# Prompt attention scores from float32r products of stacked high and low parts, in a hybrid decode-step layer

## The chip, the core and the metric

The kernel runs on one core of a Trainium2 chip. The metric is the device time of one execution in microseconds; the median of three runs is given. Engines are named as the profile names them: PE is TensorE, DVE is VectorE, ACT is ScalarE, POOL is GpSimd, SP is SyncE.

## What is computed

One transformer layer, for a prompt of 1024 tokens and for 8 sequences that each add one token to a past of 2048. The width is 1024, the feed-forward width 2816. Half of the mixer is attention with 8 query heads of 64 in 2 key groups, the other half a retention. Attention has three branches per query: compressed blocks, selected blocks, and a window of 512. For the prompt the reference does this, a block of queries at a time:

```python
qg = q.reshape(Sq, KV_GROUPS, HPG, HEAD_DIM)
s_c = jnp.einsum('sghd,ngd->sghn', qg, kcb).astype(jnp.float32) * scale
p_c = masked_softmax(s_c, (blk_end[None, :] <= q_pos[:, None])[:, None, None, :])
o_c = jnp.einsum('sghn,ngd->sghd', p_c.astype(vcb.dtype), vcb)
...
s_s = jnp.einsum('sghd,sgkd->sghk', qg, k_g).astype(jnp.float32) * scale
...
s_w = jnp.einsum('sghd,wgd->sghw', qg, kw).astype(jnp.float32) * scale
...
o = g[..., 0:1] * o_c + g[..., 1:2] * o_s + g[..., 2:3] * o_w
```

At 1024 tokens the prompt has no more selected blocks than the branch may take, so the selected branch sees every key up to the query's own. Everything is float32.

## The kernel before

Six blocks run one after another; at the end of each all engines meet at a barrier. Within a block every engine has its own instruction list, written out by hand, with semaphore counts between them.

1. `stage_project` (twice: retention columns, then keys, values and queries) multiplies the normalised rows by the input weights. Products there are "split": each float32 operand is kept as a float32r high part and a float32r rest, and `split_products` (line 374) issues three products per piece. The turned queries `qT` (4 pairs of heads x 128 rows x 1024 tokens) and keys `kselT`, `kwinT` stay in SBUF. The queries' group 0 lies in rows 0 to 63, group 1 in rows 64 to 127.
2. `stage_sequences` does the 8 single tokens. It first compresses the prompt's rows to 63 blocks (`kcbP`, `vcbP`), with weights `w1`, `w2`.
3. `stage_attention` does the prompt. Its work is 192 units in the order (tile of 128 queries, head pair, group, branch). PE's list is `EVENTS_C`: S is a unit's scores, three units ahead; T turns its exponents; V multiplies them by values; E and F close a tile. Per unit DVE takes the row maximum from PSUM, ACT writes the exponents, DVE and ACT in turn copy the turned blocks. A branch has one score area in PSUM.
4. `stage_mix_out` and `stage_feed_forward` follow, with split products throughout.

For the scores of one head, `pad_queries` copies the group's 64 rows into `qz`, whose other 64 rows are zero, so that one fp32 product over 128 rows with the keys of both groups gives the group's scores (line 1471). The masks are added by a bf16 product (line 1474). Scores are cut into pieces at PSUM banks and at the 128 columns that have a mask: for a tile t the selected branch has 128 x (t + 1) columns, the window at most 640, the compressed one 63.

```python
for lo, hi, mask in pieces(i):
    last = pe.matmul(out[:, lo:hi], m.qz[t % 2][:, hh, g, :], keys[:, lo:hi], start=True, stop=not mask)
    if mask:
        add = {"cmp": m.cmpb16[:, t, :], "causal": m.causalb, "edge": m.edgeb}[mask]
        last = pe.matmul(out[:, lo:hi], m.identb, add, start=False, stop=True)
```

`prepare_attention` runs on POOL at the end of block 2: masks to bf16, zeros, and the queries of tiles 0 and 1. Later tiles' queries are padded by POOL during block 3. In block 3 SP only loads `w_out` and the row `ln2`, for block 4. `rest_to_lo` (line 383) subtracts the high part from a float32 source; `round_to_hi` (line 379) writes the high part.

Of the kernel before, what the change touches and what calls it, by code (L numbers as in the profile page):

```python
# [16 lines left out]
F32 = mybir.dt.float32  # L17
# [44 lines left out]
KEPT = 8 * SEQ + 64 + NT * GW + 8 + 24 + 192  # L62
# [6 lines left out]
def constants():  # L69
# [23 lines left out]
    n = np.arange(63)  # L93
    put("cmp", np.stack([np.where(n[None, :] * CH + 31 <= t * P + p[:, None], 0, NEG) for t in range(TP)], 1))
# [16 lines left out]
class Semaphores:  # L111
# [5 lines left out]
    def __getitem__(self, name):  # L117
        if name not in self.by_name:
            self.by_name[name] = self.ctx.enter_context(self.nc.semaphore(name))
# [97 lines left out]
def place_kept(nc, ctx, m):  # L217
# [3 lines left out]
    m.qT = room(4 * SEQ).rearrange("p (h t) -> p h t", h=4)  # L221
    m.qbd = room(64).rearrange("p (b r) -> p b r", b=8)
    m.kselT, m.kwinT = room(SEQ), room(SEQ)
# [5 lines left out]
    m.kcbP, m.vcbP = room(64), room(128)  # L229


def place_keys(nc, ctx, m):
# [5 lines left out]
    m.qp = [m.lnb[:, 512 * i:512 * i + 512] for i in range(2)]  # L238


def place_mixer(nc, ctx, m):

    arena = ctx.enter_context(nc.sbuf_tensor("arena", [P, WORDS - CORE - KEPT], F32))
    room = Room(arena, 0)
    place_constants(m, room(NCONST - N_LATE), N_LATE)
    m.identb, m.causalb, m.edgeb = (room(P // 2).bitcast(BF16) for _ in range(3))
    m.cmpb16 = room(TP * 32).bitcast(BF16).rearrange("p (t n) -> p t n", t=TP)[:, :, 0:63]
# [13 lines left out]
    m.w2 = [b(128).rearrange("p (m n) -> p m n", m=2) for _ in range(2)]  # L261
    m.posT = [b(16) for _ in range(2)]
# [16 lines left out]
    m.rst = x(72)  # L279

# [5 lines left out]
    c = Room(arena, after_const)  # L286
    m.prob = [c(1024) for _ in range(4)]
    m.qz = [c(8 * P).rearrange("p (h g t) -> p h g t", h=4, g=2) for _ in range(2)]
# [3 lines left out]
    m.sums, m.rsc, m.nmax = [c(24), c(24)], c(24), c(8)  # L292

# [92 lines left out]
TURN_STEPS = (3, 6)  # L386


def stage_project(nc, s, m, io, first, end):
# [19 lines left out]
    with nc.Block() as block:  # L409

        @block.sync
        def _(sp):
# [13 lines left out]

            def load_x(i):
# [3 lines left out]
            if first == 0:  # L431
                load_x(0)
                sp.dma_start(m.ident, io.const[:, 0:P]).then_inc(s["ident_in"], 16)
                sp.dma_start(m.lnb, io.ln1[0:1, :].to_broadcast((P, DM))).then_inc(s["ln1_in"], 16)
# [10 lines left out]
            for n in range(n0, n1):  # L445
# [130 lines left out]
        def _(dve):  # L576
# [20 lines left out]
            if first == 0:  # L597
                dve.memset(m.small[:, 64:65], EPS).then_inc(s["a_dve_const"], 1)
                dve.wait_ge(s["ln1_in"], 16)
# [205 lines left out]
def pad_queries(pool, s, m, t):  # L805

    if t >= 2:
# [1233 lines left out]
```

## Time and profile before

| what | value |
|---|---|
| median of three runs | 2213.86 us (2211.0 to 2223.89) |
| the profiled execution | 2213.31 us, its span 2211.6 us |
| PE, PEld (weight loads) busy | 95%, 82% of the span |
| DVE, ACT, POOL busy | 35%, 27%, 21% |
| mean granted PE clock | 0.974 of full |
| line 1471 (scores), PE busy | 161.2 us, 720 records |
| line 1500 (values), line 1488 (turns) | 172.9 us, 109.7 us |
| line 374 (split products) | 855.8 and 349.7 us, 6696 records |

Busy time of PE adds up durations that overlap at their ends, so a record's duration is longer than its turn on the engine. The attention block runs from about 940 to 1316 us of the span. Its eight tiles begin their first exponent at 941.4, 957.8, 986.0, 1019.8, 1062.2, 1116.7, 1175.9 and 1238.4 us.

### The profile page before, as it was taken

To read this page: it belongs to the slowest core of one execution; us is meant where nothing else is said; L and a number is where in the kernel's file an instruction comes from. 1 tells how busy PE (TensorE), PEld (TensorE's weight loads), DVE (VectorE), ACT (ScalarE), POOL (GpSimd) and SP (SyncE) were. 2 spreads that over 40 slices of the span, in tenths; PEclk is the share of its full clock that TensorE was granted. 3 is DMA by queue.
4 is the path that set the end of the run, shared out by engine and by line. 5 is a ranking of instruction groups with operands and counts; after the bars stand their busy time and mean duration, and the time that the engine had idled before them with its cause. 6 is when DMAs were issued, how large, how long until landed. Compare 5 with 4: busy or idle time off the path is not lost. (4 is left out here: it accounts for less than half of the span.)

```text
span 2211.6 us, 34591 instructions
## 1 busy us (share of the span) xinstructions
PE 2095.4 (95%) x12669; PEld 1812.5 (82%) x12669; DVE 772.1 (35%) x1454; ACT 599.4 (27%) x1269; POOL 459.7 (21%) x433
## 2 busy tenths in 40 slices
PE   6999989978999999699999989899999999999998
PEld 5777768856776777488888868699999999999987
DVE  5544433554344444455444453301111011111015
ACT  4310112112333333265444442222110111111112
POOL 0111112212223321210000002133321333223330
PEclk9999989988999999699999989999999999999999
DMA  5211102047886773020000002121111111111123
GB/s 176 68 58 39 39 26 84 30 103 123 112 108 103 100 100 52 24 68 1 1 1 1 1 29 106 66 75 43 45 48 47 48 47 43 43 51 44 45 69 116
DMA packets 159455, 131.89 MB, mean 60 GB/s; under 512 B 15257, under 2 KB 147050, under 8 KB 159010
## 3 DMA queue, kind: packets, MB, share of 16 engines
q1 hardware_dynamic: 155234, 121.85, 23.7%
q0 software_dynamic: 4096, 8.40, 2.2%
q8 instruction: 76, 1.25, 0.2%
q14 instruction: 49, 0.40, 0.1%
HBM read 117.85 MB, written 16.55 MB: 61 GB/s over the span
## 5 line engine op out<-in xcount | busy, mean ns | idle before, releaser
L374 PE MATMUL banks<-halves 128*128 128x344 f32 (+4 forms) x5184 | 855.8, 327 | 12.6 <-POOL halves L383 12.6
L374 PEld LDWEIGHTS banks<-halves 128*128 128x128 f32 (+1 forms) x5184 | 821.2, 188 | 43.1 <-issue 7.5
L383 POOL TENSOR_TENSOR halves<-core,halves 128x1024 fp32r<-128x1024 f32 (+1 forms) x143 | 243.8, 1712 | 641.4 <-ACT halves L379 491.4
L374 PE MATMUL banks<-hidden 128*128 128x512 f32 (+3 forms) x1512 | 349.7, 387 | 9.1 <-DVE hidden L383 9.1
L374 PEld LDWEIGHTS banks<-hidden 128*128 128x128 f32 (+1 forms) x1512 | 254.7, 179 | 77.6 <-issue 9.7
L1017 PE MATMUL banks<-arena 128*128 128x254 f32 (+1 forms) x1152 | 248.4, 372 | 11.2 <-ACT arena L1148 7.1
L1017 PEld LDWEIGHTS banks<-arena 128*128 128x128 f32 x1152 | 208.8, 194 | 37.4 <-issue 6.2
L379 ACT ACTIVATE halves<-core 128x1024 fp32r<-128x1024 f32 (+1 forms) x85 | 88.1, 1047 | 388.4 <-PE banks L374 369.6
L1929 DVE TENSOR_TENSOR core<-banks,core 128x344 f32<-128x344 f32 x66 | 34.0, 516 | 440.6 <-PE banks L374 440.6
L1500 PE MATMUL banks<-kept,arena 128*128 128x64 f32 (+1 forms) x1184 | 172.9, 277 | 6.4 <-ACT arena L1532 4.2
L1500 PEld LDWEIGHTS banks<-kept,arena 128*128 128x128 f32 (+1 forms) x1184 | 151.1, 191 | 20.6 <-issue 16.9
L1471 PE MATMUL banks<-kept,arena 128*128 128x128 f32 (+4 forms) x720 | 161.2, 342 | 0.9 <-PEq L849 0.9
L1517 ACT ACTIVATE arena<-banks,arena 128x63 f32<-128x63 f32 (+8 forms) x192 | 109.5, 571 | 166.9 <-DVE arena L1570 149.7
L1570 DVE TENSOR_REDUCE arena<-banks 128x1 f32<-128x640 f32 (+4 forms) x184 | 102.4, 558 | 128.1 <-PE banks L1474 126.4
L1471 PEld LDWEIGHTS banks<-kept,arena 128*128 128x128 f32 x720 | 116.6, 192 | 32.6 <-issue 16.2
L930 POOL DMA_DIRECT2D arena<-in_cache_kv x128 | 67.8, 530 | 235.4 <-PE banks L1058 209.7
L1488 PE MATMUL banks<-core,arena 128*128 128x128 f32 (+1 forms) x592 | 109.7, 280 | 0.2 <-ACT arena L1517 0.2
L561 POOL TENSOR_TENSOR retention<-core,retention 128x256 f32<-128x256 f32 (+1 forms) x36 | 30.3, 841 | 261.4 <-ACT core L544 261.4
L1576 DVE COPY arena<-banks 63x128 f32<-63x128 f32 (+4 forms) x129 | 59.5, 461 | 62.3 <-PE banks L1488 61.2
L1148 ACT ACTIVATE arena<-banks 128x512 f32<-128x512 f32 (+1 forms) x72 | 39.7, 577 | 147.5 <-PE banks L998 147.0
L629 DVE TENSOR_TENSOR retention<-core,retention 128x128 f32<-128x128 f32 (+1 forms) x72 | 37.6, 564 | 119.9 <-ACT core L544 119.9
L1880 ACT ACTIVATE core<-banks 128x344 f32<-128x344 f32 x66 | 30.2, 458 | 175.1 <-PE banks L374 175.0
(203 smaller groups left out, 1791.2 us busy)
## 6 DMA issues: line engine op xcount, KB each, us to landing
core<-in_cache_kv SPq DMA_DIRECT2D x128, 128.0 KB, 5.5
core<-in_w_gate SPq DMA_DIRECT2D x22, 512.0 KB, 3.8
core<-in_w_up SPq DMA_DIRECT2D x22, 512.0 KB, 3.7
core<-in_x_prompt SPq DMA_DIRECT2D x16, 512.0 KB, 3.4
arena<-in_cache_kv SPq DMA_DIRECT2D x128, 64.0 KB, 5.1
arena<-in_cache_kv POOLq DMA_DIRECT2D x128, 64.0 KB, 3.9
retention<-in_w_in SPq DMA_DIRECT2D x16, 448.0 KB, 6.2
core<-in_w_down SPq DMA_DIRECT2D x16, 448.0 KB, 3.6
```

Source lines behind the costliest of these rows:

```text
L374: done = pe.matmul(out, left[a], right[b], start=(first and i == 0), stop=(last and i == 2))
L379: return act.activation(hi, x, ACT.Copy)
L383: return engine.tensor_tensor(lo, x, hi.bitcast(F32), ALU.subtract)
L930: pool.dma_start(m.selv[16 * at:16 * at + 16, half, :, :], io.pool[bass.ds(page[pg], 1), :, :, 384:512].rearrange("a c t n -> (a c) t n")) ...
L1017: last = pe.matmul(m.banks[:, 2 + mt, 0:2 * nb], m.w1[kv][:, k, P * mt:P * mt + P], m.XT[:, k % 8, :, k // 8:k // 8 + nb], start=(k == 0), ...
L1148: act.activation(m.XT.rearrange("p (h j) g c -> p j h g c", h=2)[:, i, :, :, 0:nch], m.banks[:, u % 2, :].rearrange("p (g c h) -> p h g c" ...
L1471: last = pe.matmul(out[:, lo:hi], m.qz[t % 2][:, hh, g, :], keys[:, lo:hi], start=True, stop=not mask)
L1488: last = pe.transpose(m.banks[0:w, 5 + i % 2, P * x:P * x + P], m.prob[u % 4][:, P * (first + x):P * (first + x) + w], m.ident)
L1500: last = pe.matmul(m.banks[:, 7, HD * (u % 8):HD * (u % 8) + HD], m.pts[i % 3][0:w, P * x:P * x + P], v[0:w, 64 * g:64 * g + 64], start=(f ...
L1517: act.activation(m.prob[i % 4][:, 0:width(i)], scores_of(i, width(i)), ACT.Exp, bias=m.nmax[:, i % 8:i % 8 + 1], accum_out=m.sums[UNITS[i] ...
L1570: dve.tensor_reduce(peak, out, AX.X, ALU.max, negate=True).then_inc(s["c_max"], 1)
L1576: dve.tensor_copy(m.pts[i % 3][0:w, 0:P * n], m.banks[0:w, 5 + i % 2, 0:P * n]).then_inc(s["c_kept_dve"], 1)
```

## The change

The score product of a piece becomes two float32r products. The stationary operand `qs` holds, for one head, the query's high part in rows 0 to 63 and its rest in rows 64 to 127. The moving operand is once the group's keys' high part, in both halves of the rows, and once their rest, in both halves. The two add up in PSUM to (high + rest) x (high + rest). The zero rows and `qz` go.

To lay queries and keys out in both halves, the projection block stores `qT`, `kselT` and `kwinT` to DRAM (`turned_queries`, `turned_keys`), and later blocks read them back, each group's 64 rows into both halves. Keys come in at the end of block 2 (`kstage`), queries per tile in block 3 (`qstage`). ACT writes the high parts, DVE the keys' rests, POOL the queries' rests (64 rows). The compressed keys are made in both halves by `w2twice`, which holds `w2` two times side by side. Because more semaphores are needed, 35 names that only the projection uses are cleared and freed after it, followed by a barrier of all engines. The compressed branch is 64 columns wide instead of 63. The mask casts stay on POOL; the padding there goes.

```diff
+    def retire(self, names):
+        self.nc.clear_and_free_semaphores([self.by_name.pop(name) for name in names])
+        self.nc.all_engine_barrier()
...
@@ stage_project, SP
+            def store_queries(t):
+                sp.dma_start(io.turned_queries[:, :, t * P:(t + 1) * P].rearrange("h p t -> p h t"),
+                             m.qT[:, :, t * P:(t + 1) * P]).then_inc(s["turned_out"], 16)
...
+                if ch in (5, 6) and t == 2:
+                    sp.wait_ge(s["tkept"], turns_before(n))
+                    sp.dma_start(io.turned_keys[ch - 5], (m.kselT, m.kwinT)[ch - 5]).then_inc(s["turned_out"], 16)
+                if kind == "q" and t >= 2:
+                    sp.wait_ge(s["tkept"], turns_before(n - 1))
+                    store_queries(t - 2)
...
+                sp.wait_ge(s["tkept"], turns_before(NI - 1))
+                store_queries(TP - 1)
                 sp.wait_ge(s["gate_done"], NT)
                 sp.dma_start(io.gate_rows, m.gates[0:NB_SEQ, TP, :]).then_inc(s["rows_out"], 16)
                 sp.wait_ge(s["rows_out"], 32)
+                sp.wait_ge(s["turned_out"], 16 * (2 + TP))
...
@@ stage_sequences, SP
                 sp.dma_start(m.w2[kv], io.w2[kv]).then_inc(s[f"b_w_in{kv}"], 16)
+                if kv == 0:
+                    for half in range(2):
+                        sp.dma_start(m.w2twice[:, :, HD * half:HD * half + HD], io.w2[0]).then_inc(s["b_w_in0"], 16)
...
+            sp.wait_ge(s["b_grouped"], 2 * (NB_SEQ + 1))
+            for what in range(2):
+                for g in range(2):
+                    for half in range(2):
+                        sp.dma_start(m.kstage[what][g][HD * half:HD * half + HD, :],
+                                     io.turned_keys[what, HD * g:HD * g + HD, :]).then_inc(s["c_keys_in"], 16)
...
@@ stage_sequences, POOL
-            prepare_attention(pool, s, m)
+            pool.wait_ge(s["const_in"], 48)
+            for b16, f32 in stored_masks(m):
+                pool.tensor_copy(b16, f32).then_inc(s["c_masks"], 1)
+            pool.wait_ge(s["c_masks"], 4)
...
@@ stage_attention, SP
+            def load_queries(t):
+
+                for g in range(2):
+                    src = io.turned_queries[:, HD * g:HD * g + HD, P * t:P * t + P].rearrange("h d t -> d h t")
+                    for half in range(2):
+                        sp.dma_start(m.qstage[t % 2][HD * half:HD * half + HD, g, :, :], src
+                                     ).then_inc(s[f"c_q_in{t % 2}"], 16)
+
+            for t in range(2):
+                load_queries(t)
+            sp.wait_ge(s["c_keys_lo"], 4)
             for k in range(NSLOT):
                 load_w_out(sp, s, m, io, k)
+            for t in range(2, TP):
+                sp.wait_ge(s["c_queries"], t - 1)
+                load_queries(t)
...
@@ stage_attention, PE
-                    pe.wait_ge(s["c_queries"], 2 * t + 2)
+                    pe.wait_ge(s["c_queries"], t + 1)
+                    if t == 0 and hh == 0 and br:
+                        pe.wait_ge(s["c_keys_lo"], 2 * g + br)
...
                     for lo, hi, mask in pieces(i):
-                        last = pe.matmul(out[:, lo:hi], m.qz[t % 2][:, hh, g, :], keys[:, lo:hi], start=True, stop=not mask)
+                        for v in range(2):
+                            last = pe.matmul(out[:, lo:hi], m.qs[t % 2][:, g, hh, :], pair[v][:, first + lo:first + hi],
+                                             start=(v == 0), stop=(v == 1 and not mask))
...
@@ stage_attention, ACT
+            def queries_hi(t):
+
+                act.wait_ge(s[f"c_q_in{t % 2}"], 64 * (t // 2 + 1))
+                wait(act, "c_scores", PER_TILE * (t - 1))
+                round_to_hi(act, m.qs[t % 2], m.qstage[t % 2]).then_inc(s["c_q_hi"], 1)
+
+            queries_hi(0)
+            act.wait_ge(s["c_keys_in"], 128)
+            for g in range(2):
+                for what in range(2):
+                    round_to_hi(act, m.keys[what][g][0], m.kstage[what][g]).then_inc(s["c_keys_hi"], 1)
+            queries_hi(1)
...
+                    t = i // PER_TILE + 1
+                    if i % PER_TILE == 4 and 2 <= t < TP:
+                        queries_hi(t)
                     act.wait_ge(s["c_max"], i + 1)
...
@@ stage_attention, POOL
+            def queries_lo(t):
+
+                pool.wait_ge(s["c_q_hi"], t + 1)
+                low = slice(HD, P)
+                rest_to_lo(pool, m.qs[t % 2][low], m.qstage[t % 2][low], m.qs[t % 2][low]).then_inc(s["c_queries"], 1)
+
+            queries_lo(0)
+            pool.wait_ge(s["c_queries"], 1)
+            queries_lo(1)
+            for t in range(TP - 1):
+                if t:
+                    pool.wait_ge(s["c_weighted"], t)
+                    queries_lo(t + 1)
...
@@ stage_attention, DVE
+            for g in range(2):
+                for what in range(2):
+                    dve.wait_ge(s["c_keys_hi"], 2 * g + what + 1)
+                    rest_to_lo(dve, m.keys[what][g][1], m.kstage[what][g], m.keys[what][g][0]).then_inc(s["c_keys_lo"], 1)
             for what, i in EVENTS_C:
...
@@ build, after stage_project
+            s.retire(PROJECT_ONLY)
```

## Rows read from the trace of the kernel before

**Rows 1.** Stretches of the span by engine; us, busy us (records), granted clock, DMA.
```profile
918.00:928.00 10.00, 0.91 (x8) 0.58 (x7) 8.61 (x12) 3.38 (x5) 6.83 (x9) 0.61 0.01 5
...
936.00:940.00 4.00, 3.23 (x23) 2.11 (x21) 0.60 (x3) 0.00 (x0) 0.00 (x0) 0.85 0.00 0
941.00:957.80 16.80, 16.23 (x139) 14.09 (x138) 10.18 (x44) 12.61 (x62) 0.77 (x2) 1.00 0.81 220
1238.40:1303.50 65.10, 64.52 (x469) 53.84 (x467) 30.56 (x47) 28.12 (x69) 2.76 (x1) 1.00 0.00 1
```

**Rows 2.** Groups by shape, TensorE, attention stage: records, busy us, mean ns.
```profile
L1471 PE MATMUL banks<-kept,arena 128*128 128x128 f32 x368 | 67.5, 276 | 0.0
...
L1471 PE MATMUL banks<-kept,arena 128*128 128x384 f32 x112 | 47.1, 502 | 0.0
...
L1471 PE MATMUL banks<-kept,arena 128*128 128x512 f32 x64 | 32.8, 594 | 0.0
...
L1471 PE MATMUL banks<-kept,arena 128*128 128x63 f32 x128 | 21.4, 249 | 0.9 <-PEq L849 0.9
...
L1471 PE MATMUL banks<-kept,arena 128*128 128x256 f32 x48 | 14.3, 380 | 0.0
```

**Rows 3.** Timeline, three stretches of TensorE: start, us, operation, records merged.
```profile
1273.08 0.19 PEld L1471 LDWEIGHTS banks<-kept,arena 128*128 128x128 f32 x1 [0.24 <-issue]
1273.51 0.51 PEld L1471 LDWEIGHTS banks<-kept,arena 128*128 128x128 f32 x2 [0.24 <-issue]
...
1107.37 1.28 PE L1500 MATMUL banks<-kept,arena 128*128 128x64 f32 x10
1108.49 0.28 PE L1488 MATMUL banks<-core,arena 128*128 128x128 f32 x1
...
336.93 5.80 PE L374 MATMUL banks<-hidden 128*128 128x512 f32 x24
342.56 0.27 PE L738 MATMUL banks<-core 128*128 128x128 f32 x1
```

**Rows 4.** Stretches, line 374 alone: 344 columns, then 256; busy us (records).
```profile
1500.00:1550.00 50.00, 50.00 (x320) 50.00 (x319) 1.00 0.18 52
...
2158.00:2161.00 3.00, 3.00 (x26) 3.00 (x27) 1.00 0.00 0
```

**Rows 5.** Line 374's weight loads: records, ns min/median/max, shapes.
```profile
L374 PEld LDWEIGHTS banks<-halves x5184: 87/188/338, 1321.1 to 2197.2; 128*128 128x128 f32 x198, 128*8 128x8 f32 x2
```

**Rows 6.** Timeline, first maximum and SyncE's first issues of the attention stage.
```profile
940.93 0.22 DVE L1567 TENSOR_REDUCE arena<-banks 128x1 f32<-128x63 f32 x1 [0.95 <-PE banks L1474]
...
940.26 4.98 SPq L1420 DMA_DIRECT2D core<-in_w_out  x8
```

**Rows 7.** Issues by line: count, KB each, median us from issue to landing.
```profile
arena<-in_cmp_w_k SPq DMA_DIRECT2D x8, 256.0 KB, 3.9
```

**Rows 8.** Timeline, the same splitting operations on three engines, next stage's start.
```profile
1316.52 7.68 ACT L379 ACTIVATE halves<-core 128x1024 fp32r<-128x1024 f32 x8 [0.29 <-PEq L1451]
...
1317.61 1.22 DVE L383 TENSOR_TENSOR halves<-core,halves 128x1024 fp32r<-128x1024 f32 x1 [3.25 <-ACT halves L379]
1319.50 4.89 DVE L383 TENSOR_TENSOR halves<-core,halves 128x1024 fp32r<-128x1024 f32 x3 [0.67 <-ACT halves L379]
...
1318.60 2.44 POOL L383 TENSOR_TENSOR halves<-core,halves 128x1024 fp32r<-128x1024 f32 x1 [68.56 <-ACT halves L379]
```

**Rows 9.** Timeline, end of the projection stage and the next stage's first issue.
```profile
450.64 0.68 DVE L652 TENSOR_SCALAR kept<-banks 128x512 f32<-128x512 f32 x1
...
457.98 0.39 DVE L656 TENSOR_SCALAR kept<-banks 64x32 f32<-64x32 f32 x2 [0.75 <-PE banks L738]
458.66 0.24 SPq L853 DMA_DIRECT2D arena<-in_page_table  x1
```

**Rows 10.** Groups by line: one operation in 905 to 940, and the whole span.
```profile
L1332 DVE TENSOR_SCALAR core<-core 8x30 f32<-8x30 f32 x1 | 1.7, 1691 | 0.0
...
L1332 DVE TENSOR_SCALAR core<-core 8x30 f32<-8x30 f32 x8 | 6.9, 858 | 0.3
```

More of the change, by code:

```diff
@@ L92, in constants @@
     put("edge", np.where(i[None, :] > p[:, None], 0, NEG))
-    n = np.arange(63)
-    put("cmp", np.stack([np.where(n[None, :] * CH + 31 <= t * P + p[:, None], 0, NEG) for t in range(TP)], 1))
+    n = np.arange(64)
+    put("cmp", np.stack([np.where((n[None, :] < 63) & (n[None, :] * CH + 31 <= t * P + p[:, None]), 0, NEG)
+                         for t in range(TP)], 1))
     r = np.arange(NRANK)
@@ L228, in place_kept @@
     m.gs = room(24).rearrange("p (b n) -> p b n", b=8)
-    m.kcbP, m.vcbP = room(64), room(128)
+    m.vcbP = room(128)
+    m.identb, m.causalb, m.edgeb = (room(P // 2).bitcast(BF16) for _ in range(3))
+    m.cmpb16 = room(TP * 32).bitcast(BF16).rearrange("p (t n) -> p t n", t=TP)
+    m.kcbP = ctx.enter_context(nc.sbuf_tensor("kept_pairs", [P, CMPK], F32R, side="right"))[:, :].rearrange(
+        "p (g v n) -> p g v n", g=2, v=2)
 def place_keys(nc, ctx, m):
@@ L279, in place_mixer @@
     m.rst = x(72)
+    m.kstage = [[m.pool[:, 2048 * a + 1024 * g:2048 * a + 1024 * g + 1024] for g in range(2)] for a in range(2)]
     m.S0, m.S2, m.rsq = scores[:, 0:4096], sel, sel[:, 0:1024]
@@ L283, in place_mixer, with place_attention @@
     m.R4 = m.kwb[:, 0:256].rearrange("p (j e) -> p j e", j=4)
-    c = Room(arena, after_const)
+def place_attention(nc, ctx, m):
+    room = Room(ctx.enter_context(nc.sbuf_tensor("pairs", [P, PAIRS_C], F32R)), 0)
+    m.keys = [[[room(SEQ) for _ in range(2)] for _ in range(2)] for _ in range(2)]
+    m.qs = [room(SEQ).rearrange("p (g h t) -> p g h t", g=2, h=4) for _ in range(2)]
+    c = Room(ctx.enter_context(nc.sbuf_tensor("softmax", [P, WORDS - CORE - KEPT - CMPK - PAIRS_C], F32)), 0)
     m.prob = [c(1024) for _ in range(4)]
-    m.qz = [c(8 * P).rearrange("p (h g t) -> p h g t", h=4, g=2) for _ in range(2)]
+    m.qstage = [c(SEQ).rearrange("p (g h t) -> p g h t", g=2, h=4) for _ in range(2)]
     m.pts = [c(512) for _ in range(3)]
@@ L292, in place_mixer @@
     m.sums, m.rsc, m.nmax = [c(24), c(24)], c(24), c(8)
+    m.kstage = [[m.pool[:, 2048 * a + 1024 * g:2048 * a + 1024 * g + 1024] for g in range(2)] for a in range(2)]
 def place_feed_forward(nc, ctx, m):
@@ L386 @@
 TURN_STEPS = (3, 6)
+PROJECT_ONLY = ("x_in0", "x_in1", "ident_in", "aw_in", "aw_hi", "aw_lo", "turned", "hT_hi", "hT_lo", "h_done", "rms_done",
+                "raw_done", "roped", "tkept", "tturned", "cos_done", "proj_done", "vkept", "w_used", "att_done",
+                "att_masked", "kd_done", "o_done", "state_done", "state_out", "gates_kept", "gates_late", "gate_done",
+                "turned_out", "rows_out") + tuple(f"slot_out{k}" for k in range(5))
 def stage_project(nc, s, m, io, first, end):
@@ L1433, in width @@
     def width(u):
-        return 63 if UNITS[u][3] == 0 else P * key_tiles(u)
+        return 64 if UNITS[u][3] == 0 else P * key_tiles(u)
     def pieces(u):
@@ L1543, in _ @@
         def _(pool):
[L1544 to L1549 removed]
+            def queries_lo(t):
[9 more added lines that the diff above has]
+                    queries_lo(t + 1)
+                pool.wait_ge(s["c_queries"], t + 2)
                 pool.wait_ge(s["c_inverted"], t + 1)
@@ L2014, in build @@
                     stage_project(nc, s, m, io, 4, NCH)
-            place_mixer(nc, kept, m)
-            stage_sequences(nc, s, m, io)
-            stage_attention(nc, s, m, io)
+            s.retire(PROJECT_ONLY)
+            with ExitStack() as part:
+                place_mixer(nc, part, m)
+                stage_sequences(nc, s, m, io)
+            with ExitStack() as part:
+                place_attention(nc, part, m)
+                stage_attention(nc, s, m, io)
         place_feed_forward(nc, ctx, m)
```

96 lines of the change are left out of this document (49 added, 47 removed).

## The prediction

> **What bounds the kernel now.** I read first the stretches of the span by engine, because the change touches four stages and a price holds only in its own stage. The last tile of the prompt's attention, 1238.4 to 1303.5, is the picture to keep [rows 1]: TensorE is busy 64.52 of 65.10 us at the full clock, VectorE 30.56 and ScalarE 28.12. So in this stage a shorter TensorE instruction shortens the stage, and ScalarE and VectorE have about half their time free. At the stage's head and tail another thing decides: the chain from the first scores to the first maximum, and what must be ready before them.
>
> **The score products.** By shape, the stage has 720 records of line 1471 [rows 2]. There are 360 products in the code, so an fp32 product runs as two records, each with its own weight load. After the change each piece is two float32r products, which run as one record each (line 374 has 5184 records for the 5184 float32r products that its loops issue). The count of records and loads stays 720; only the length of a record changes.
>
> The length is the distance between starts, not the duration, because records overlap. Two neighbouring loads of 512-column fp32 records start at 1273.08 and 1273.51: 0.43 us apart [rows 3]. By columns that is 0.323 for 384, 0.216 for 256, and 0.108 for 128. For float32r, 24 records of 512 columns fill the 5.63 us from 336.93 to the next group at 342.56, 0.235 each [rows 3]; 320 records in 50 us, of 344 columns, are 0.156, and 26 in 3 us, of 256, are 0.115 [rows 4]. Between 344 and 512, 384 columns come to 0.175.
>
> - 512 columns: 64 x (0.43 - 0.235) = 12.5 us
> - 384 columns: 112 x (0.323 - 0.175) = 16.6 us
> - 256 columns: 48 x (0.216 - 0.115) = 4.8 us
>
> The 128-column records, 368 of them, are the unknown: float32r at 128 columns does not occur before. By stream alone it would take 0.235/4 = 0.059 instead of 0.11. But an fp32 record of 64 columns streams as long as a float32r record of 128, and ten of those fill the 1.12 us from 1107.37 to 1108.49: 0.112 [rows 3]. Something other than the stream sets that floor; the load is the candidate, since a float32r load lasts 188 ns with 128 columns and 87 with 8 [rows 5], about 0.10 us for the columns. I take 0.11, no gain, by that nearest row; the ends are 0.059 (368 x 0.052 = 19 us more gained) and, if load and stream followed one another, 0.10 + 0.059 = 0.16 (18 us lost). The 63-column records (now 64 columns) go with them.
>
> The Trainium skill has a rule that speaks against the change: TensorE: Matmul & The Clock Gate, in its part on packing small matmuls ("The mechanism"), says that a weight load overlaps matmuls in flight only when it targets another row group, and these all use the whole array. By it no load here would be hidden, and the change would lose time. The 0.156 us of 344 columns contradicts it: load 0.10 and stream 0.235 x 344/512 = 0.158 would add up to 0.26. I go by the row, and keep the rule as a rival.
>
> Sum of the wide records: 33.9 us. Not all will show: where scores come back sooner, some steps will end on an exponent or a copy. With two engines at half load I take 31; the ends are 33.9 and half.
>
> **The start of the attention stage.** Before, the first maximum runs at 940.93, 0.67 us after SyncE's first issue of the stage at 940.26 [rows 6]; queries were padded by GpSimd under the sequences' tail. Now the chain starts inside the stage. Four query loads of 128 KB go first on SyncE. Eight issues took 4.98 us there, 0.62 apart [rows 6], so the fourth goes out at 942.1; 256 KB landed 3.9 us after issue [rows 7]: 946.0. ScalarE rounds eight 1024-column slices in 7.68 us in the stage after [rows 8], 0.95 apart: queries until 947.1, four key parts until 950.9, the second tile's queries until 951.9. GpSimd's rest of 1024 columns takes 2.44 [rows 8], so 949.5 and 954.3. VectorE has four key rests to do before its first maximum, in program order: 1.22 each, but the one that met GpSimd's ended 1.1 after GpSimd did, and three took 4.89 instead of 3.7 [rows 8]. The first rest meets the first queries' (ends 950.6), the second and third end at 953.0, the fourth meets the second tile's queries or not: 954.2 to 956.4. Against 940.93 that is 13.3 to 15.5 us late; I take 14. The first scores are earlier than that (951); maxima, exponents and turns are what is late.
>
> Meanwhile TensorE is idle. Before, it had nearly no work from 918 to 928 (0.91 us busy); the granted clock was 0.61 on average there and still 0.85 in 936 to 940 [rows 1]. So once it had fallen from 2.4 to 1.2 GHz, it came back only some 8 us after the work did. Tile 0 keeps TensorE occupied: 139 records x 0.11 = 15 of its 16.8 us [rows 1], so 8 us at half clock cost at most 4, some of it in its gaps: 3 us. Nothing excludes 0 or 5.
>
> **The rest.**
> - ScalarE rounds the queries of six more tiles, 0.95 each, one place before an exponent; ScalarE is free for half the tile [rows 1], so most is hidden; uncovered, it is 6 x 0.95 = 5.7. I take 1. GpSimd's part runs a tile ahead; SyncE's query loads wait for GpSimd two tiles earlier and hold up only w_out and the ln2 row, which nothing needs until the next stage.
> - Project stage: SyncE stores turned keys and queries in its queue. Behind its waits stand the prompt rows (needed only in the next stage) and the gate rows. The last query tile is copied at 451.3 (450.64 + 0.68), the stage's last copy ends at 458.4 (457.98 + 0.39) [rows 9]; a 256 KB store, issue and the 3.9 us of [rows 7], lands by 456. Hidden, by 2 us; without that cover, 2 to 4 us.
> - Clearing 35 semaphores, and one more barrier: the trace shows none; the next row is a stage change, 458.37 to the next issue at 458.66 [rows 9], 0.3 us. I take five of that, 1.5, with ends at one and ten, 0.3 and 3.
> - Sequences: two more w2 loads ahead of the position rows and of w1 of the values: 2 x 0.5 us of issue, partly hidden: 0.5. The 2 MB of keys are read once GpSimd has grouped the last rows and SyncE has sent the last window values, under the last sequence's softmax; without that cover they would be late by up to their own landing time. GpSimd's padding leaves VectorE's last chain, in which one 8x30 operation took 1691 ns [rows 10], against 858 on average over eight with that one in it: -0.9 us.
>
> Sum: -31 + 14 + 3 + 1 + 0 + 1.5 + 0.5 - 0.9 = -11.9 us. The profiled execution took 2213.31 (its span 2211.6 and 1.7 around it), against a median of 2213.86: 2201.4 us, and I say 2201. Half a per cent, 11 us, is about what a measurement of this kernel can tell from no change.
>
> **Rivals.**
> A. The sum, with a start between 11 and 20 us in all and the gain between 28 and 34: 2192 to 2209. Chance 0.58.
> B. The narrow records quicken too, because the float32r load is shorter than its duration says: 19 us more, 2182. Against it stands the 64-column row. 0.10.
> C. TensorE stops being the bound: score, maximum, exponent in turn set the pace, and only half of the 33.9 comes: 2201 + 14 = 2215. For it: at 1024 columns maximum and exponent follow one another, and one bank group serves each branch. Against it: half-idle engines, and three units' work between a score and its turn. 0.12.
> D. The clock stays at half through tile 0 and into tile 1: some 12 us more, 2213. For it: the start is thinner than the tail in which the clock fell before. 0.11.
> E. The other side: weight loads are not hidden under float32r records here. Each record then costs 0.10 plus its stream: 64 x 0.095 + 112 x 0.048 + 48 x 0.001 - 368 x 0.05 = -7 us, and the 128 of 64 columns lose 0.02 each against 0.11, 3: the products lose 10 instead of gaining 31, 2242. It decides for slower from about 0.03 us of load showing per record (23 us over 720). Spacing at 344 columns speaks against it. 0.09.
>
> **How the numbers follow.** A lies below 2203 in about two thirds: 0.38, with B 0.48 faster; the rest of A with C and D, 0.43, is within 0.5%; E, 0.09, slower. The range takes in A, C, D and part of B: 2186 to 2217.
>
> **What would show it.** Two float32r records per piece, 720, with 512 columns 0.23 apart and 128 columns 0.11; the first maximum 14 to 16 us after the stage's first issue; half clock in the first tile; tiles 4 to 7 each 5 to 8 us shorter, tiles 0 and 1 no shorter but for their start. The prediction is wrong if narrow records stand at 0.06 or 0.16, if late tiles shrink by less than 3 us, or if the first maximum comes after 20 us.

## The result, and the profile after

The changed kernel takes 2225.55 us (median of 20 runs, 2222.85 to 2233.49) against 2213.72 for the kernel before (20 runs): a ratio of 1.006, 95% interval 1.005 to 1.0071, so 12 us slower, where 2201 had been forecast. The profiled execution took 2224.61 us, its span 2222.9, its mean granted clock 0.954 (0.974 before).

The first thing to read is where in the span the two kernels part. Each tile runs here from its first exponent to the next tile's (the last tile to its last exponent), in us:

| stretch | before | after | difference |
|---|---|---|---|
| end of projection to first issue of the sequences | 0.28 | 3.24 | +3.0 |
| end of the sequences' last group of eight products to the first exponent | 2.36 | 16.82 | +14.5 |
| tile 0 | 16.4 | 26.4 | +10.0 |
| tile 1 | 28.2 | 45.1 | +16.8 |
| tile 2 | 33.8 | 34.3 | +0.5 |
| tiles 3 to 7 together | 283.7 | 252.8 | -30.9 |

The rest is projection (+1.2), sequences (-3.2) and what follows the last exponent (-0.6). The first two move as much from one execution to the next: in the profiled executions below, of either kernel's code, projection ends between 457.3 and 459.6 and the sequences last 474.5 to 481.6 us.

So the late tiles gained what had been said, the start lost what had been said, and two tiles in which nothing was to be won or lost but the 3 us of the clock lost 27. Stretches of the changed kernel, to be read against [rows 1] (span of the stretch, busy us and records of PE, PEld, DVE, ACT and POOL, granted clock, DMA):

```profile
940.00:945.00 5.00, 0.22 (x1) 0.13 (x1) 0.59 (x3) 0.00 (x0) 0.00 (x0) 1.00 0.30 88
945.00:950.00 5.00, 0.19 (x1) 0.22 (x2) 1.78 (x1) 3.82 (x5) 2.34 (x1) 0.50 0.41 122
...
956.80:983.20 26.40, 25.97 (x131) 24.33 (x132) 10.31 (x42) 13.37 (x62) 0.00 (x0) 0.50 0.66 160
983.20:1028.30 45.10, 45.10 (x222) 43.01 (x221) 15.48 (x41) 18.32 (x65) 5.11 (x2) 0.50 0.04 12
1028.30:1035.00 6.70, 6.70 (x35) 6.47 (x34) 2.33 (x7) 2.60 (x9) 0.00 (x0) 0.50 0.01 4
1035.00:1062.60 27.60, 27.60 (x240) 26.56 (x239) 14.90 (x32) 18.18 (x59) 5.12 (x2) 0.96 0.07 20
1256.20:1315.40 59.20, 57.80 (x466) 54.86 (x465) 30.53 (x47) 28.12 (x69) 2.76 (x1) 0.97 0.00 1
```

The clock falls to half (0.50, 1.2 GHz) at 945, while TensorE waits, and is still there at 1035. Through tile 1 and the head of tile 2 TensorE is busy without a gap (45.10 of 45.10, 6.70 of 6.70), and VectorE and ScalarE are less busy per microsecond than before. In tile 1 nothing is waited for: the same 222 records take 45.1 us in place of the 28.2 of the kernel before:

```profile
957.80:986.00 28.20, 26.95 (x222) 24.51 (x221) 14.74 (x41) 16.16 (x64) 4.13 (x4) 0.94 0.00 1
```

By the 0.96 from 1035 on the clock is back at about 1037, 92 us after it fell. Tile 7 at 59.2 against 65.1 is the change as it was meant.

The start, by the timeline of the same kernel, answers to [rows 6, 8]:

```profile
941.19 5.22 SPq L1507 DMA_DIRECT2D softmax<-turned_queries  x8
946.18 1.06 ACT L398 ACTIVATE pairs<-softmax 128x1024 fp32r<-128x1024 f32 x1 [18.51 <-DMA softmax<-turned_queries]
947.14 3.88 ACT L398 ACTIVATE pairs<-core 128x1024 fp32r<-128x1024 f32 x4
947.32 2.34 POOL L402 TENSOR_TENSOR pairs<-softmax,pairs 64x1024 fp32r<-64x1024 f32 x1 [23.70 <-ACT pairs L398]
948.22 8.08 DVE L402 TENSOR_TENSOR pairs<-core,pairs 128x1024 fp32r<-128x1024 f32 x4 [7.29 <-ACT pairs L398]
949.81 0.61 PE L1535 MATMUL banks<-kept_pairs,pairs 128*128 128x64 f32 x2 [9.27 <-POOL pairs L402]
...
956.33 0.23 DVE L1659 TENSOR_REDUCE softmax<-banks 128x1 f32<-128x64 f32 x1
```

The first maximum stands 15.1 us after SyncE's first issue, behind the four rests that VectorE takes in program order; TensorE waits 9.27 us for the queries and, behind the first scores, another 4.4 for the first exponent.

The score records of the whole stage by shape (records, busy us, mean ns) answer to [rows 2]:

```profile
L1535 PE MATMUL banks<-pairs 128*128 128x128 f32 x368 | 76.0, 306 | 0.7 <-DVE pairs L402 0.7
...
L1535 PE MATMUL banks<-pairs 128*128 128x384 f32 x112 | 33.0, 376 | 0.0
...
L1535 PE MATMUL banks<-kept_pairs,pairs 128*128 128x64 f32 x128 | 28.9, 312 | 9.3 <-POOL pairs L402 9.3
...
L1535 PE MATMUL banks<-pairs 128*128 128x512 f32 x64 | 23.0, 440 | 0.0
```

With the 48 of 256 columns the counts are the 720 that were expected, shape by shape. 512 columns went from 594 to 440 ns and 384 from 502 to 376; 128 columns went from 276 to 306, a mean that holds the half-clock tiles too.

At the stage change behind the projection, timeline again, against [rows 9]:

```profile
457.98 0.67 DVE L688 TENSOR_SCALAR turned_rows<-banks 128x512 f32<-128x512 f32 x1
458.68 0.36 SPq L451 DMA_DIRECT2D turned_queries<-turned_rows  x1
...
459.08 0.40 SPq L513 DMA_DIRECT2D gate_rows<-kept  x1
459.21 0.39 DVE L692 TENSOR_SCALAR kept<-banks 64x32 f32<-64x32 f32 x2 [0.56 <-PE banks L774]
462.84 0.25 SPq L870 DMA_DIRECT2D arena<-in_page_table  x1
```

The last query tile leaves VectorE at 458.65, not at 451.3, and its store is issued 4.2 us before the next stage can begin.

### The profile page after: what moved, and what is told of

Read it like the earlier page. It is cut to its first block and busy times, and to the rows that moved or that the text cites. A ratio compares the mean times of both kernels' runs of the same rounds, so it can differ in the third digit from the quotient of the medians.

```text
span 2222.9 us, 34694 instructions
## 1 busy us (share of the span) xinstructions
PE 2093.9 (94%) x12669; PEld 1844.6 (83%) x12669; DVE 779.3 (35%) x1460; ACT 613.2 (28%) x1282; POOL 469.1 (21%) x424
## 5 line engine op out<-in xcount | busy, mean ns | idle before, releaser
L1565 PE MATMUL banks<-kept,softmax 128*128 128x64 f32 (+1 forms) x1184 | 188.2, 293 | 6.1 <-ACT softmax L1612 4.3
L1565 PEld LDWEIGHTS banks<-kept,softmax 128*128 128x128 f32 (+1 forms) x1184 | 166.7, 208 | 15.6 <-issue 8.2
L1597 ACT ACTIVATE softmax<-banks,softmax 128x64 f32<-128x64 f32 (+8 forms) x192 | 109.6, 571 | 141.8 <-DVE softmax L1662 133.1
L1662 DVE TENSOR_REDUCE softmax<-banks 128x1 f32<-128x640 f32 (+4 forms) x184 | 102.5, 558 | 112.8 <-PE banks L1539 111.8
L1553 PE MATMUL banks<-core,softmax 128*128 128x128 f32 (+1 forms) x592 | 119.4, 298 | 4.4 <-ACT softmax L1597 4.4
L1535 PE MATMUL banks<-pairs 128*128 128x128 f32 (+3 forms) x592 | 121.9, 336 | 0.7 <-DVE pairs L402 0.7
L1535 PEld LDWEIGHTS banks<-pairs 128*128 128x128 f32 x592 | 104.7, 219 | 3.7 <-issue 1.0
L1553 PEld LDWEIGHTS banks<-core,softmax 128*128 128x128 f32 (+1 forms) x592 | 79.5, 165 | 9.2 <-ACT softmax L1597 4.6
L1668 DVE COPY softmax<-banks 64x128 f32<-64x128 f32 (+4 forms) x129 | 59.4, 460 | 73.3 <-PE banks L1553 72.9
```

The source lines that it names most:

```text
L1535: last = pe.matmul(out[:, lo:hi], m.qs[t % 2][:, g, hh, :], pair[v][:, first + lo:first + hi], start=(v == 0), stop=(v == 1 and not mask))
L1553: last = pe.transpose(m.banks[0:w, 5 + i % 2, P * x:P * x + P], m.prob[u % 4][:, P * (first + x):P * (first + x) + w], m.ident)
L1565: last = pe.matmul(m.banks[:, 7, HD * (u % 8):HD * (u % 8) + HD], m.pts[i % 3][0:w, P * x:P * x + P], v[0:w, 64 * g:64 * g + 64], start=(f ...
L1597: act.activation(m.prob[i % 4][:, 0:width(i)], scores_of(i, width(i)), ACT.Exp, bias=m.nmax[:, i % 8:i % 8 + 1], accum_out=m.sums[UNITS[i] ...
L1662: dve.tensor_reduce(peak, out, AX.X, ALU.max, negate=True).then_inc(s["c_max"], 1)
L1668: dve.tensor_copy(m.pts[i % 3][0:w, 0:P * n], m.banks[0:w, 5 + i % 2, 0:P * n]).then_inc(s["c_kept_dve"], 1)
```

## The experiments

**1. TensorE kept occupied at the start.** The question was whether the wait, the products, or both cost the clock.

```
 pe.wait_ge(s["c_masks"], 4)
+def occupy(n):
+    for _ in range(n):
+        pe.matmul(m.banks[:, 6, 0:P], m.ident, m.ident, start=True, stop=True)
+occupy(56)          # and occupy(16) behind the third unit's scores
```

> Three theories of the 27 us that tiles 0 and 1 lost at a granted clock of 0.50. Stall: TensorE's wait at the stage's start drops the clock, and no narrow product brings it back. Thin: the wait drops it, and it is the narrow float32r products that do not bring it back, where fp32 ones did. Own: the narrow float32r products drop the clock by themselves, wait or no wait. Here TensorE multiplies the identity by itself 56 times before the first scores and 16 times before the first turn (fp32, into a bank that nothing reads), the rest as in the changed kernel. Stall and Thin: the clock stays at 1.00, tile 0 takes 16 to 18 us and tile 1 28 (first exponent to first exponent) in place of 26.4 and 45.1, and the run comes to 2195 to 2201. Own: the clock falls to 0.50 within tile 0 or 1 all the same, and the time is 2215 to 2226.

Measured: 2210.96 us (10 runs, 2188.49 to 2216.9), ratio 0.9983, 0.9957 to 1.001, between the two figures named. The stretches of its profiled execution (2208.61 us):

```profile
940.00:954.30 14.30, 14.30 (x132) 14.30 (x131) 8.54 (x7) 5.79 (x7) 5.50 (x2) 1.00 0.26 75
954.30:971.60 17.30, 16.97 (x151) 15.71 (x150) 9.45 (x42) 12.53 (x62) 0.00 (x0) 1.00 0.99 243
971.60:980.00 8.40, 7.35 (x66) 6.81 (x64) 5.70 (x15) 5.02 (x20) 5.04 (x2) 1.00 0.02 5
980.00:1011.40 31.40, 31.33 (x155) 29.97 (x155) 9.45 (x27) 12.49 (x46) 0.07 (x1) 0.50 0.06 17
```

Tile 0 is back at 17.3 us, at the full clock: that loss was the wait's. Tile 1 takes 39.8 us, because the clock falls again at 980. The timeline shows what came just before:

```profile
977.68 1.91 DVE L1699 TENSOR_REDUCE softmax<-softmax 128x512 f32<-128x1536 f32 x1 [0.84 <-POOL softmax L1648]
...
980.07 0.89 PE L1573 MATMUL banks<-kept,softmax 128*128 128x64 f32 x4 [1.12 <-DVE softmax L1676]
```

VectorE sums tile 0's outputs for 1.91 us, a turn's copy queues behind it, and TensorE waits 1.12 us. The run decides against Own for tile 0; for tile 1 it leaves open whether that short wait or the products did it. Nor does the wait lead to it every time, it seems: the run of 2188.49 us has a mean granted clock of 0.975, the other nine 0.963 to 0.968.

**2. The kernel before, started late.** The other side of the same question: the wait without the float32r products.

```
+for _ in range(12):
+    own.after(dve.tensor_tensor(m.prob[3], m.kselT, m.kwinT, ALU.add))
 for what, i in EVENTS_C:
```

> The kernel before, with twelve additions of 1024 columns on VectorE ahead of its first maximum (into a buffer that is overwritten later), so that its softmax starts about 14.6 us late, as in the changed kernel, while its products stay fp32. Stall: the clock falls to 0.50 and stays there through tiles 0 and 1 as in the changed kernel: 14.6 and another 20 to 27 us, 2248 to 2255. Thin and Own: fp32 products bring the clock back within tile 0: 14.6 and at most 5 more, 2228 to 2233.

Measured: 2238.96 us (4 runs), ratio 1.0112, 1.0093 to 1.0131. Neither figure was met:

```profile
942.00:956.90 14.90, 0.64 (x6) 0.40 (x5) 14.45 (x15) 0.00 (x0) 0.00 (x0) 0.60 0.91 246
956.90:984.70 27.80, 27.29 (x131) 24.04 (x131) 10.39 (x43) 13.39 (x61) 1.16 (x2) 0.50 0.00 1
984.70:990.00 5.30, 5.30 (x42) 4.71 (x42) 3.20 (x11) 3.30 (x14) 1.15 (x2) 0.89 0.01 3
990.00:1013.70 23.70, 22.44 (x184) 20.56 (x184) 11.56 (x30) 12.93 (x51) 2.60 (x3) 0.93 0.00 1
```

A late start alone takes the clock down and costs tile 0 11.4 us over the 14.5 of the start, with fp32 products too. But tile 1 has 0.89 over its first 5 us, so the clock is back at about 986, and takes 29.0 us: the fp32 kernel gets its clock back one tile earlier than the changed one. From there on all tiles are as before to 0.02 us.

**3. fp32 products in tiles 0 and 1 of the changed kernel.**

```
-for v in range(2):
-    last = pe.matmul(..., m.qs[t % 2][:, g, hh, :], pair[v][...], ...)
+if br and t < 2:
+    last = pe.matmul(out[:, lo:hi], m.qs[t % 2][:, g, hh, :].bitcast(F32),
+                     m.kstage[br - 1][g][:, first + lo:first + hi], start=True, stop=not mask)
+else: ...
```

The compressed branch stays float32r. SyncE's loads of `w_out` also wait here until tile 1 has its scores, so the products are not the only difference.

> The changed kernel, but in tiles 0 and 1 the scores of the selected and the window branch are one fp32 product each, of the stacked queries with the unsplit keys, which lie twice one above the other in the staging buffer (so high + low query times the whole key: the same scores); w_out loads wait until tile 1 has its scores. The stage starts as late as in the changed kernel. Stall: the clock stays at 0.50 through tiles 0 and 1, 2221 to 2228. Thin: the clock comes back within tile 0, tile 0 takes at most 21 us and tile 1 28, and it stays up in tile 2: 2197 to 2204. Own: the same in tiles 0 and 1, but it falls again in tile 2 at float32r products of 128 to 384 columns: 2204 to 2215.

Measured: 2207.94 us (10 runs, 2203.43 to 2212.69), ratio 0.9973, 0.9961 to 0.9984.

```profile
955.00:982.60 27.60, 27.09 (x131) 23.83 (x132) 10.40 (x43) 13.37 (x62) 0.00 (x0) 0.50 0.14 39
982.60:1005.00 22.40, 22.40 (x109) 20.38 (x109) 8.69 (x22) 9.42 (x31) 5.11 (x2) 0.50 0.00 1
1005.00:1018.00 13.00, 13.00 (x117) 12.13 (x116) 6.53 (x20) 8.31 (x34) 0.00 (x0) 1.00 0.00 1
1018.00:1048.20 30.20, 30.20 (x271) 29.02 (x271) 17.22 (x39) 20.46 (x67) 5.13 (x2) 1.00 0.58 141
```

It beats the changed kernel by 18 us and lies in Own's range, but neither Own nor Thin holds as it was put: the clock does not fall in tile 2, and tile 0 takes 27.5 us at half clock. The clock returns at 1005, well inside tile 1, where the float32r products had needed until 1037, and tile 2 runs whole at 1.00, in 30.2 us against 33.8 before.

**4. A shorter start.** ScalarE rounds the keys first, which lie ready, and the queries when they land.

```
-queries_hi(0)
 act.wait_ge(s["c_keys_in"], 128)
 ...
-queries_hi(1)
+queries_hi(0)       # the second tile's queries inside tile 0
```

> The changed kernel with the stage's start reordered: ScalarE rounds the four key parts first (they are in by then) and the first queries after, and the second tile's queries inside tile 0. VectorE's four rests then lie under the queries' landing: first maximum at 950 to 951.5 in place of 956.3. Stall: TensorE still waits some 9 us; if that is enough to drop the clock the tiles lose the same 27 us and the time is 2217 to 2220, if not 2191 to 2196. Thin and Own: the clock is at 0.50 in tiles 0 and 1 as before, 2217 to 2220.

Measured: 2224.2 us (10 runs: three at 2215.4 to 2218.4, seven at 2223 to 2225.9). The profiled execution is one of the three:

```profile
940.00:949.50 9.50, 1.14 (x7) 1.17 (x7) 5.01 (x6) 4.95 (x5) 2.33 (x1) 0.71 0.61 171
949.50:975.90 26.40, 26.40 (x135) 24.76 (x134) 10.48 (x42) 14.44 (x62) 2.34 (x1) 0.50 0.58 138
```

The first maximum came at 949.08, 6.1 us earlier against the end of the sequences, and the clock fell all the same; tiles 0 and 1 take the same 26.4 and 45.1 us. In the profiled execution the 6 us show in the end; the median gives only 1.4 of them, less than the two kernels can be told apart. The other seven have a mean granted clock of 0.952 to 0.954 against 0.957 in the three, so they stood longer at half clock; where was not profiled.

**5. and 6. What happens in tile 1.** Occupied as in the first experiment, once with fp32 products in tiles 0 and 1, once with float32r throughout and the wait of tile 1 filled:

```
+elif what == "F" and i < 2:
+    for _ in range(6):
+        pe.matmul(m.banks[:, 3, 0:P], m.ident, m.ident, start=True, stop=True)
```

> Both edits together: TensorE occupied through the stage's start (56 and 16 identity products) and fp32 products with the unsplit keys in tiles 0 and 1. With TensorE occupied alone the profiled execution kept the clock at 1.00 through tile 0, but a wait of 1.12 us at 980 us was followed by 0.50 until tile 2, and tile 1 took 39.8 us. Theory Thin (float32r products of 128 and 256 columns don't bring the clock back, fp32 ones do soon): tile 1 28 to 30 us, tile 2 30 to 31, 2193 to 2198 us. Rival (the wait at tile 1's sum alone decides, whatever the products): tile 1 38 to 41 us, 2206 to 2211.

> TensorE occupied through the stage's start as in the first experiment, and six identity products more at the place in tile 1 (and one in tile 2) where TensorE waited 1.12 us for VectorE's sum over tile 0. All products float32r. Theory Gap (a wait drops the clock and the thin products only fail to bring it back): clock 1.00 through tiles 0 to 2, tile 1 28 to 29 us, 2190 to 2195. Theory Own (thin float32r products let the clock fall without any wait): tile 1 still 36 to 42 us, 2203 to 2212.

Measured: 2193.83 us (4 runs, ratio 0.9916, 0.99 to 0.9933) and 2191.38 us (4 runs, 0.9904, 0.9888 to 0.9921). Stretches of tiles 1 and 2 of the one with fp32:

```profile
972.10:998.70 26.60, 25.32 (x221) 23.19 (x221) 14.70 (x41) 16.71 (x65) 5.12 (x2) 1.00 0.00 1
998.70:1028.90 30.20, 30.20 (x271) 29.02 (x271) 17.20 (x39) 20.48 (x67) 5.13 (x2) 1.00 0.60 141
```

and of tiles 0, 1 and 2 of the one with float32r and the filled wait:

```profile
954.90:972.20 17.30, 16.98 (x151) 15.73 (x150) 9.45 (x42) 12.50 (x62) 0.00 (x0) 1.00 1.01 242
972.20:998.50 26.30, 26.09 (x234) 24.76 (x233) 14.75 (x41) 16.72 (x66) 5.13 (x2) 1.00 0.08 23
998.50:1030.10 31.60, 31.60 (x284) 30.43 (x284) 17.41 (x39) 20.46 (x68) 5.13 (x2) 1.00 0.06 18
```

Own falls: with no wait ahead of them the narrow float32r products run whole tiles at 1.00. And the short wait matters: with fp32 products TensorE waits 1.00 and 0.27 us in tile 1 and keeps its clock, with float32r 1.12 us lost it for 41 us in the first experiment; filled, it is kept. The kernel before and the second experiment have the same two waits in tile 1 (0.99 and 0.26 us, 1.00 and 0.26), and there the clock falls too, but for 3.4 us only (the 0.74 and 0.87 named in the eleventh expectation, the 0.93 in the second experiment's last row). That speaks for the products; one trace of each kernel cannot show that they alone make the difference.

**7. The shorter start with both fillings** (40 and 10 identity products at the start, six in each of the two waits).

> The start reordered (keys rounded first, first maximum near 949 in place of 956.3), TensorE occupied there (40 and 10 identity products) and in the wait of tile 1 and tile 2. If the clock stays at 1.00 the gain of the shorter start shows in full: 5 us below the kernel with the same fillings and the old start, 2184 to 2190, faster than both kernels by over 1%. If the clock falls all the same in tile 0 or 1: 2200 to 2212.

Measured: 2186.99 us (4 runs, 2185.27 to 2193.55), ratio 0.9893, 0.9873 to 0.9914. The median is 4.4 us below that of the sixth experiment, for a first maximum 5.4 us earlier; three of the four runs lie below all four of that one and the fourth, 2193.55, above, so the two intervals overlap.

**8. The stage change.** Gate rows stored as soon as they stand, last query store left out.

```
+sp.wait_ge(s["gate_done"], NT)
+sp.dma_start(io.gate_rows, ...)
 sp.wait_ge(s["tkept"], turns_before(NI - 1))
-store_queries(TP - 1)
```

> The changed kernel, which at the end of the project stage stores the last prompt tile's turned queries at 458.68 and the gate rows at 459.08 and starts the next stage at 462.84, 3.24 us after the last copy of the stage (0.28 before). Here the gate rows are stored as soon as the last gates stand and the last query store is left out (tile 7 reads tile 6's queries, so its scores are those of other queries). Store theory: the landing of the last query store sets the 3.24 us; the stage change falls to 0.5 to 1.5 us and the run gains 2 to 2.5 us. Clear theory (35 semaphores cleared and one more barrier): it stays above 2.5 us, no gain.

The timeline at the end of the stage:

```profile
451.80 0.40 SPq L511 DMA_DIRECT2D gate_rows<-kept  x1
...
457.84 0.39 DVE L691 TENSOR_SCALAR kept<-banks 64x32 f32<-64x32 f32 x2 [0.57 <-PE banks L773]
459.85 0.25 SPq L869 DMA_DIRECT2D arena<-in_page_table  x1
```

From the last copy's end, 458.23, to the first issue are 1.62 us, against 3.24 with the store and 0.28 before. So the late store, with the gate rows behind it, costs 1.6 us. The 1.3 that are left are put down to clearing the semaphores and the barrier; no run took those away alone. Both theories had half. The total, 2228.47 us, does not show it: with the clock at half in tiles 0 and 1 again, runs lay between 2222.4 and 2232.

**9. and 10. What brings the clock back.** In the changed kernel with its late start, TensorE gets one unbroken burst inside tile 0: 40 float32r products of 512 columns, or 90 of 128 columns, their result unused; tile 1's wait is filled in both.

```
+if what == "S" and i == 6:
+    for _ in range(40):                       # or 90
+        pe.matmul(m.banks[:, 3, 0:512], m.keys[0][0][0][:, 0:P],      # or 0:P
+                  m.keys[0][0][0][:, 0:512], start=True, stop=True)
```

> The changed kernel with its late start left as it is, six identity products in the wait of tile 1 and of tile 2, and ahead of tile 0's seventh unit 40 float32r products of 512 columns whose result nothing reads (19 us at half clock, 9.4 at full). What brings the clock back, after it fell: theory Long records: it is 1.00 before the burst ends (burst 10 to 15 us) and stays there through tiles 0 and 1, which get 8 and 17 us shorter: 2206 to 2214. Rival (it comes back only after some 80 us whatever is issued): 0.50 through the burst and tiles 0 and 1, 2225.6 + 19 = 2240 to 2247.

> As the kernel with the 512-column burst, but 90 float32r products of 128 columns in its place (19 us at half clock too, without a break, 9.9 at full). Long records: the clock stays at 0.50 in the burst and until tile 2, 2240 to 2247. Rival (an unbroken stretch of TensorE work brings it back, of whatever length of record): as with 512 columns, 2206 to 2214.

Measured: 2202.79 us (5 runs, ratio 0.9953, 0.9938 to 0.9969) and 2228.27 us (4 runs, 1.0061, 1.0041 to 1.0081). The burst of 512 columns on the timeline (start, us):

```profile
960.12 11.29 PE L1526 MATMUL banks<-pairs 128*128 128x512 f32 x40
```

the stretches of that kernel from the burst's start:

```profile
960.10:963.00 2.90, 2.90 (x9) 2.32 (x9) 0.06 (x1) 0.61 (x3) 0.00 (x0) 0.50 1.04 229
963.00:967.00 4.00, 4.00 (x17) 3.19 (x16) 0.00 (x0) 0.00 (x0) 0.00 (x0) 0.85 1.03 241
967.00:971.40 4.40, 4.40 (x23) 3.66 (x22) 0.00 (x0) 0.00 (x0) 0.00 (x0) 1.00 1.11 300
971.40:984.80 13.40, 13.08 (x117) 11.96 (x116) 7.74 (x34) 9.84 (x47) 0.00 (x0) 1.00 0.22 43
984.80:1011.30 26.50, 26.29 (x235) 24.88 (x234) 14.77 (x41) 16.84 (x66) 5.11 (x2) 1.00 0.08 21
```

the burst of 128 columns on its kernel's timeline:

```profile
962.46 19.44 PE L1526 MATMUL banks<-pairs 128*128 128x128 f32 x90
```

and the stretches of that kernel:

```profile
962.40:970.00 7.60, 7.60 (x38) 7.60 (x38) 0.10 (x1) 0.61 (x3) 0.00 (x0) 0.50 1.03 250
970.00:981.90 11.90, 11.90 (x58) 11.90 (x57) 0.00 (x0) 0.00 (x0) 0.00 (x0) 0.50 0.57 133
```

Some 4 us into the 512-column products (0.85 over 963 to 967) the clock is at 1.00, and it stays there through the rest of tile 0 and tile 1. After 19.44 us of 128-column products, without a gap, it is still at 0.50. 11 us of useless work, with tile 1's wait filled, made the changed kernel 23 us faster, to 3 us below the expectation. The second run came out 12 us below its expectation: its tile 1 was at half for only 13 us, and it got its clock back at about 1017.5. Just before that lies the filling of tile 1's wait, twelve fp32 records of 128 columns:

```profile
1014.51 2.88 PE L1561 MATMUL banks<-core 128*128 128x128 f32 x12
...
1015.00:1036.60 21.60, 21.60 (x184) 20.62 (x183) 10.56 (x29) 11.87 (x45) 0.00 (x0) 0.94 0.09 25
```

So 512 columns may not be needed; whether these twelve records raised the clock, one trace cannot say. With float32r products throughout and no burst or filling behind the fall, it came back in tile 2, the first with score records of 256 columns: 8 to 10 us after that tile's first exponent in the changed kernel and in the first, fourth and eighth experiments, when it had been down for 92, 41, 85 and 92 us. In the first experiment, where tile 2 begins at 1011.4:

```profile
1020.00:1046.00 26.00, 26.00 (x229) 24.86 (x228) 13.78 (x30) 16.40 (x54) 3.63 (x2) 0.98 0.08 22
```

That does not fit the rival that it comes back after some 80 us whatever is issued.

**11. A control:** the filled waits of tiles 1 and 2 in the kernel before.

> A control: the kernel before with the six identity products in the waits of tiles 1 and 2. Its granted clock was 0.74 at 966 to 970 and 0.87 at 970 to 975 and 1.00 else, so it can gain some 2 us: 2209 to 2214. If more (below 2205), part of what the fillings gave the changed kernel has nothing to do with the change.

Measured: 2213.71 us (10 runs), ratio 1.0004, 0.9994 to 1.0014. Tile 1 took 26.7 us in place of 28.2 and tile 2 35.2 in place of 33.8, where it had no wait to fill. The kernel before has nothing to win from the fillings.

**12. The first tile's queries loaded a stage earlier**, into a part of the slot pool that the last sequence is done with, and the second key group's rests behind the first three maxima.

> The kernel with the shorter start and both fillings, and besides the first tile's queries loaded in the stage before (into the part of the slot pool that the last sequence no longer uses), rounded first on ScalarE, and VectorE's rests of the second key group placed after the first three maxima. Fillings cut to 18 and 6 products. First maximum 5 to 7 us after the stage's start, where the shorter start had 9.4: 3 to 4 us less, 2181 to 2186, if the clock stays at 1.00 through tiles 0 and 1. If the shorter filling lets it fall: 2200 to 2212.

Measured: 2185.72 us (4 runs: 2183.93, 2184.68, 2186.76 and 2201.49), ratio 0.9898, 0.9858 to 0.9938. The first maximum came at 947.26, 7.0 us after the sequences' last group of products in place of the shorter start's 10.7. Against the seventh experiment the median is 1.3 us lower, less than the two can be told apart; the run at 2201 fits the outcome named for a clock that falls, and its mean granted clock is 0.966 against 0.974 and 0.975 in the others, but it was not profiled.

## Why the prediction was wrong

- **The score products, -31.** Right in the sum, not term by term. Tiles 3 to 7 gained 30.9 us, after losing 1.5 to a short fall of the clock in tile 7 (the 0.97 above). With the clock held (sixth experiment, tile 2 from the fifth) tiles 2 to 7 gain 3.6 and 32.4 us, 36.0: more than the 33.9 that the prediction had as the upper end, so that 30.9 meets 31 partly by luck. By the distances between starts in tiles 3 to 7 of the sixth experiment, the wide records give 26.2 us there, where the prediction's lengths make 30.7, and the turns beside them, for which it had no term, 8.8. The 128-column records went from 0.111 to 0.100; tile 1 takes 26.3 us against 26.7 in the control, both filled and at the full clock, and tile 0 17.3 against 17.5 with fp32 products behind the same filling (fifth experiment). So 128 columns quicken next to nothing, as taken from the 64-column row, and no engine took over as the bound (rivals B and C fall).
- **Rival E and its rule.** At the full clock the records of the 512-column burst start 0.227 us apart (median in the trace), each with a load of its own that lasts 0.188. That is close to the 0.235 of the prediction's row, and no load shows beside the stream. The Trainium skill (TensorE: Matmul & The Clock Gate, "The mechanism") says that a weight load overlaps matmuls in flight only when it targets another row group. These whole-array products do not bear that out; the same section names a background weight buffer as another way to overlap. The score products lie between: 0.271 apart at 512 columns and 0.210 at 384 in those tiles, where 0.235 and 0.175 had been taken. What the 0.04 are stays open; a load that shows in part is one candidate. The 128-column burst at half clock has 0.216 each (19.44 by 90), 0.108 at the full clock: the floor of 0.11 that was taken, neither the stream alone (0.059) nor load and stream in turn (0.16). With the sum of the products at a gain of over 30 us, E falls.
- **The start, +14.** Right: 14.5. The rests on VectorE took 8.08 us for four, the queries landed at 946.2.
- **The clock, +3: the step that failed.** The prediction said that tile 0 keeps TensorE occupied, so that 8 us at half clock cost at most 4. Tile 0 did keep it occupied (25.97 of 26.40 us), and the clock stayed down for 90 us: 10.0 us in tile 0, 16.8 in tile 1, and the 3.6 that tile 2 should have won and 0.5 more, some 31 us where 3 had been put. Rival D had the mechanism, at 0.11, but its 12 us are less than half the price. The 8 us came from a row of another stage, with other records in it [rows 1]. The ninth and tenth experiments show that what follows the wait decides how long the clock stays down: behind 512-column products it was up after some 4 us, behind 128-column ones not in 19. The change put a wait in front of the tiles with the narrowest score records. Filled, the wait costs its own 14 us and no more.
- **fp32 or float32r.** The second experiment shows that the late start alone costs the old products 12 us more in tiles 0 and 1. The changed kernel lost 27 behind a wait of the same length, and got its clock back at 1037, against 986 there and 1005 in the third experiment. The prediction had no term for that. The 19 us between the two runs with fp32 products, and what makes an fp32 record of 128 columns better than a float32r one, have no cause here; fp32 products alone did not raise the clock in all 27.8 us of the second experiment's tile 0.
- **The project stores, +0.** Wrong by 1.6 us: the copy at 450.64 [rows 9] is not that of the last query tile, which is copied some 6 us later (456.56 before, 457.98 after), and the gate rows stand in the queue behind its store. The **clear and the barrier, +1.5**, are 1.3 at most, what the eighth experiment leaves.
- **The rest** (ScalarE's queries, w2, GpSimd's relief) is too small to be read off; the sequences' length varies by more.

Measured between the two profiled spans: 1.2 (projection) + 3.0 (stage change) - 3.2 (sequences) + 14.5 (start) + 27.3 (tiles 0 to 2) - 30.9 (tiles 3 to 7) - 0.6 (what follows) = +11.3 us, against -11.9 in the forecast. The difference is the clock's but for a few microseconds.

## What to carry to other kernels

A stall of TensorE must be priced twice, by its length and by what the work behind it does to the granted clock; take the second from a stretch with the same records, not from another stage. Here the stretch had the narrowest score records of the stage, and the second price was twice the first. Where the wait can't be removed, cheap products that keep TensorE supplied through it were worth more here than an earlier start: the changed kernel is 0.6% slower than the kernel before, with both waits filled 1.0% faster, and 1.1% with the start shortened too.

## What the runs showed of the hardware

- The granted clock stayed at 0.50 from 983 to 1035 of the changed kernel with TensorE busy in every one of these 52 us, and in the tenth experiment 19.44 us of unbroken 128-column float32r products did not raise it, where in the ninth some 4 us of 512-column ones did.
- A wait of 1.12 us was followed by 41 us at half clock in one execution (float32r products), and waits of 0.99 to 1.00 us at the same place by 3.4, 3.4 and none in three others (fp32 products). The Trainium skill (TensorE: Matmul & The Clock Gate, "HAM oscillation — how this bites in real kernels") says that a wait for data lets the clock fall, and advises an order of the work that leaves the engine no such wait. With the waits filled the clock stayed up in these runs (2225.55 to 2191.38 us), which agrees.
- Shortening the stall by 6.1 us without removing it gave 1.4 us in the median, no more than the noise; shortening it by 5.4 with the clock held gave 4.4, with intervals that overlap.
